# Squaring steps of a recurrent mixer on four TensorE tiles instead of two

## The chip, the cores and the metric

One core of a Trainium2 chip runs the whole kernel. The metric is the device time of one execution in microseconds. TensorE multiplies matrices into PSUM; VectorE (DVE) and ScalarE (ACT) take the products out of PSUM, change them and write them to SBUF; SyncE and GpSimd only move data here. TensorE is used as 64 by 64 tiles in the part that is changed: which half of the partitions an operand lies on gives the tile's row, and which half of the partitions of PSUM the result goes to gives its column, so that there are four tiles, (0,0), (0,1), (1,0) and (1,1).

## What is computed

A two-layer encoder on 512 + 256 tokens of width 1024. A layer is a SwiGLU, a mixer of three kinds of heads, and another SwiGLU. The change is in the first kind of heads, the RWKV-7 scan, four heads of 64 channels, run forward and backward:

```python
def step(s, inp):
    r_t, w_t, k_t, v_t, kk_t, a_t = inp
    s = (s * w_t[:, :, None, :]
         - jnp.einsum('bhij,bhj->bhi', s, kk_t)[..., None] * (kk_t * a_t)[:, :, None, :]
         + v_t[..., None] * k_t[:, :, None, :])
    return s, jnp.einsum('bhij,bhj->bhi', s, r_t)
```

The kernel does it by chunks of 64 tokens. For each chunk and head it needs the inverse of a 64 by 64 triangular matrix. It splits it into blocks of 16 on the diagonal, whose inverse is the product (I+N)(I+N^2)(I+N^4)(I+N^8), and the rest. The squaring steps of this product are what the change touches.

## The kernel before

**Stages.** In each layer the mixer's recurrent part, `rwkv`, runs four passes (`q` = 0 to 3: two directions times two pairs of heads). A pass holds 12 chunks for 2 heads, and goes through eleven steps (`s` = 0 to 10). Each step is done for three groups (`g` = 0, 1, 2) of four chunks one after another, so a pass is 33 calls of `batch(l, q, s, g)`, written once for each engine: the one of TensorE multiplies (L948 on), the ones of ScalarE (L1511 on) and VectorE (L1976 on) take the products out. Group g has the two PSUM banks 2g and 2g+1 for itself.

**Order.** Every engine runs its own list in order. A product of step s waits until VectorE and ScalarE have both finished step s-1 of its group (`rv` and `ra_` at `s - 1`); both of them wait for TensorE's products of their step (`rp`). While group 0 is taken out, TensorE multiplies groups 1 and 2.

**Layouts.** A 64 by 64 matrix of a chunk and a head lies on one half of the partitions. In one layout the half tells the head, in the other the parity of the chunk. `into_pairs` reads the half by head and writes the half by parity, `out_of_pairs` the other way round; both walk over the four tiles of `TILES`. `inside` reads and writes the same half, so it uses the tiles (0,0) and (1,1) alone. `out_of_pairs` can already add a second product to the first in PSUM. In steps 3 to 6 all is in the layout by parity. Step 3 squares (`sq_b`, `sq_a`) and gives N^2 as `M2X[..., 0, :]` and its transpose as `sq_c`; `M2X[..., 1, :]` is the running product X.

- Step 4: from `sq_c` times `M2X`, both parts side by side in 128 columns, bank 2g gets N^4 and the addend to X, and bank 2g+1 the transpose of N^4. ScalarE copies the transpose to `sq_b` (L1520); VectorE copies N^4 to `sq_a` (L2005) and adds the addend to X in SBUF (L2006).
- Step 5: the same once more with `sq_b`, `sq_a`. ScalarE copies the transpose of N^8 to `sq_c` (L1522); VectorE adds to X (L2008).
- Step 6: the last addend, from `sq_c` and X, added by VectorE (L2008).
- Step 7: two `out_of_pairs` calls; ScalarE takes them out in three copies (L1524 to L1526), VectorE waits for the first of them (`turned`), and adds the unit matrix (L2010).

Each of the float32 products appears in the trace as two weight loads and two matmuls.

**Beside the steps.** After group 0 of some steps TensorE has other work (`lora_part` in steps 2 to 5 of passes 0 to 2, `chain_step` in pass 2, means, variances and a "bonus" product in pass 3, from `between`). ScalarE has a sigmoid after each of steps 2 to 5. VectorE computes the next pass's features after steps 6 to 9: `cumulate` (L2025 to L2030) stands right behind step 6 on its list. In pass 3 it has `bonus` (L2143) behind group 0 and three operations on 128x768 (L2132, L2135, L2177) behind steps 4 and 5.

Of the kernel before, what the change touches and what calls it, by code (L numbers as in the profile page):

```python
# [40 lines left out]
CH = 64  # L41
# [3 lines left out]
TILES = ((0, 0), (1, 1), (0, 1), (1, 0))  # L45
# [92 lines left out]
def build(nc, xT, wa, par_d, small_d, const_d, hy_d, hw_d, bias_d, outT):  # L138
# [4 lines left out]
    with ExitStack() as ctx:  # L143
# [617 lines left out]
        def _(pe):  # L761
# [157 lines left out]
                    if i == 0 and s == 0:  # L919
                        norm()  # L920

            def into_pairs(g, n, at, width, lhs, rhs):

                for j in range(2):
                    for h, p in TILES:
                        c, r = 4 * g + 2 * j + p, slice(64 * h, 64 * h + 64)
                        m = mm(ps[64 * p:64 * p + 64, 2 * g + h, width * j + at:width * j + at + n], lhs(c)[r, :], rhs(c)[r, :])
                return m

            def out_of_pairs(g, n, at, width, lhs, rhs, lhs2=None, rhs2=None):  # L930
# [17 lines left out]
            def batch(l, q, s, g):  # L948
# [3 lines left out]
                part = lambda t, a: (lambda c: t[:, c, a, :])  # L952
                parts = lambda t, a, n: (lambda c: t[:, c, a:a + n, :].rearrange("p a t -> p (a t)"))
                vv = lambda v: vtok[:, i, v, :]
                if s:
                    if s - 1 in VECTOR_STAGES:
                        pe.wait_ge(*rv.at(l, "b", q, s - 1, g))
                    if s - 1 in ACT_STAGES:
                        pe.wait_ge(*ra_.at(l, "b", q, s - 1, g))
                elif q:  # L960
                    pe.wait_ge(*rv.at(l, "b", q - 1, BATCH - 1, g))
                    pe.wait_ge(*ra_.at(l, "b", q - 1, BATCH - 1, g))
# [8 lines left out]
                    inside(g, 1, 64, 0, one(sq_a), one(sq_b))  # L971
                    m = inside(g, 1, 64, 256, part(Q, 0), vv)
                elif s == 4:
                    inside(g, 0, 128, 0, one(sq_c), parts(M2X, 0, 2))
                    m = inside(g, 1, 64, 0, part(M2X, 0), one(sq_c))
                elif s == 5:
                    inside(g, 0, 64, 0, one(sq_b), part(M2X, 1))
                    m = inside(g, 1, 64, 0, one(sq_a), one(sq_b))
                elif s == 6:
                    m = inside(g, 0, 64, 0, one(sq_c), part(M2X, 1))  # L980
                elif s == 7:
                    out_of_pairs(g, 64, 192, 256, part(NR, 0), part(M2X, 1))
                    m = out_of_pairs(g, 192, 0, 256, part(M2X, 1), parts(NR, 0, 3))
                elif s == 8:
                    into_pairs(g, 64, 0, 192, one(sq_a), one(sq_b))
                    m = into_pairs(g, 128, 64, 192, part(NR, 0), parts(Q, 0, 2))
                elif s == 9:
                    m = inside(g, 0, 128, 0, one(sq_c), parts(NR, 1, 2))
                else:
                    out_of_pairs(g, 128, 0, 256, part(Q, 0), parts(btok_Mrb, 0, 2))  # L990
                    out_of_pairs(g, 64, 128, 256, part(btok_Mrb, 0), part(Q, 1), one(ktok), vv)
                    m = out_of_pairs(g, 64, 192, 256, part(Q, 1), part(btok_Mrb, 1), vv, one(Mrk))
# [387 lines left out]
        def _(sa):  # L1380
# [130 lines left out]
            def batch(l, q, s, g):  # L1511
# [5 lines left out]
                    sa.copy(sq_c[:, h, :], same(o + 1, 0))  # L1517
                    m = A(NR[:, h, 2, :], ps[:, o + 1, 256:512].rearrange("p (v t) -> p v t", t=CH), ACT.Copy, scale=-1.0)
                elif s == 4:
                    m = sa.copy(sq_b[:, h, :], same(o + 1, 0))  # L1520
                elif s == 5:
                    m = sa.copy(sq_c[:, h, :], same(o + 1, 0))  # L1522
                elif s == 7:
                    sa.copy(outer(sq_b[:, h, :]), quad(o, 256, 192)).then_inc(*ra_.inc(l, "turned", q, g))  # L1524
                    sa.copy(outer(sq_a[:, h, :]), quad(o, 256, 0))
# [222 lines left out]
        def _(ve):  # L1748
# [227 lines left out]
            def batch(l, q, s, g):  # L1976
# [5 lines left out]
                X = M2X[:, h, 1, :]  # L1982
                if s == 7:
                    ve.wait_ge(*ra_.at(l, "turned", q, g))
                else:
                    ve.wait_ge(*rp.at(*k, s, g))
                if s:
# [14 lines left out]
                elif s == 3:  # L2002
                    m = ve.tensor_copy(M2X[:, h, 0, :], same(o, 0))
                elif s == 4:
                    ve.tensor_copy(sq_a[:, h, :], same(o, 0, CH, 2 * CH))  # L2005
                    m = TT(X, X, same(o, CH, CH, 2 * CH), AD)  # L2006
                elif s in (5, 6):
                    m = TT(X, X, same(o, 0), AD)  # L2008
                elif s == 7:
                    m = TT(NR[:, h, 0, :], sq_b[:, h, :], eye_b(4), AD)  # L2010
# [508 lines left out]
```

## Time and profile before

| | |
|---|---|
| median of three executions | 3546.54 us (3543.47 to 3546.89) |
| profiled execution | 3548.5 us, of which its span is 3546.7 us |
| TensorE busy with matmuls | 3405.4 us, 96% of the span |
| VectorE busy | 1797.2 us, 51% |
| ScalarE busy | 978.5 us, 28% |
| mean granted TensorE clock | 0.99 |
| recurrent part | about 846 to 1022 us and 2600 to 2775 us of the span |

A profiled execution lists every instruction with its start, its length and what ended the idle time before it. In the timeline view, instructions of one kind are merged into one row: the row has the first start, the time to the last end, the engine (PE is the matmul side of TensorE, PEld its weight loads, which overlap), the line of the kernel, output and inputs by name, shapes and the count. "<-DVE" in brackets says that a wait for VectorE ended there; "<-issue" means idle time for which the profile shows nothing that was waited for. All products have line L767, that of a helper, and are told apart by the names of their operands.

### The profile page before, as it was taken

What the parts mean: (1) busy time and instruction counts of PE and PEld (TensorE: products, weight loads), DVE (VectorE), ACT (ScalarE), POOL (GpSimd) and SP (SyncE); (2) the same over time, 40 slices, a digit from 0 to 9 for tenths busy, and PEclk for the clock granted to TensorE, in tenths of its full rate; (3) what the DMA queues carried; (4) which work ended last, traced back from release to release, by engine and by line L of the source; (5) the groups of instructions that cost most, each with busy time, mean ns of one, the idle gap of its engine ahead of it and who ended that gap; (6) DMA issues with size and microseconds to landing.
All of it is one profiled execution on the core that took longest, in us unless ns stands there. A gap on an engine that the chain in (4) does not pass through costs nothing.

```text
span 3546.7 us, 60872 instructions
## 1 busy us (share of the span) xinstructions
PE 3405.4 (96%) x26620; PEld 3217.2 (91%) x26620; DVE 1797.2 (51%) x3152; ACT 978.5 (28%) x1607; POOL 50.5 (1%) x62
## 2 busy tenths in 40 slices
PE   7999999999887999999999999999998879999998
PEld 7999999887766999999999999998877669999998
DVE  5443445664878433333454434456448774333334
ACT  4221223222453321211331212232134633221212
POOL 0000000000000000000000000000000000000000
PEclk9999999999998999999999999999999989999999
DMA  3222121231051212212122221222300512122121
GB/s 136 62 70 77 57 72 63 97 109 58 4 196 50 88 54 69 65 62 73 56 78 74 67 76 54 77 96 67 121 26 21 209 48 71 59 71 61 52 72 62
DMA packets 78456, 264.30 MB, mean 75 GB/s; under 512 B 8738, under 2 KB 8738, under 8 KB 76912
## 3 DMA queue, kind: packets, MB, share of 16 engines
q1 hardware_dynamic: 74640, 248.08, 21.2%
q0 software_dynamic: 3552, 12.34, 1.1%
q8 instruction: 210, 3.44, 0.4%
q14 instruction: 54, 0.44, 0.0%
HBM read 230.50 MB, written 29.88 MB: 73 GB/s over the span
## 4 chain that ended last, share of the span: by engine, by line
PE 90%; DVE 6%; ACT 2%; issue 1%; DMA 0%; SPq 0%; DVEq 0%
PE ps L767 89%; DVE uv L2228 1%; PE ps L1285 1%; DVE rstd L1779 0%; DVE sc L2281 0%; DMA x<-xT 0%; DVE Mrk L1995 0%; ACT Q L1526 0%; ACT L1398 0%; DVE xab L2217 0%; DVE btok_Mrb L1991 0%; DVE btok_Mrb L1992 0%; DVE ktok L1996 0%; DVE xab L2218 0%; DVE sc L2292 0%
## 5 line engine op out<-in xcount | busy, mean ns | idle before, releaser
L767 PE MATMUL ps<-hh,wh 128*128 128x384 f32 (+2 forms) x3520 | 1188.8, 338 | 11.9 <-DVE hl L1787 10.9
L767 PE MATMUL ps<-hl,wh 128*128 128x384 f32 (+2 forms) x3520 | 1179.9, 335 | 0.0
L767 PE MATMUL ps<-hh,wl 128*128 128x384 f32 (+2 forms) x3520 | 1179.4, 335 | 0.0
L767 PEld LDWEIGHTS ps<-hh,wh 128*128 128x128 f32 x3520 | 663.5, 188 | 35.5 <-issue 16.5
L767 PEld LDWEIGHTS ps<-hl,wh 128*128 128x128 f32 x3520 | 663.8, 189 | 15.3 <-issue 0.3
L767 PEld LDWEIGHTS ps<-hh,wl 128*128 128x128 f32 x3520 | 663.6, 189 | 14.3
L1413 ACT CAST wh<-wring 128x1024 fp32r<-128x1024 f32 (+2 forms) x372 | 346.1, 955 | 660.8 <-PE ps L767 654.8
L767 PE MATMUL ps<-act_high,wl 128*128 128x384 f32 x1408 | 470.3, 334 | 0.0
L767 PE MATMUL ps<-act_high,wh 128*128 128x384 f32 x1408 | 470.3, 334 | 0.0
L767 PE MATMUL ps<-act_low,wh 128*128 128x384 f32 x1408 | 470.3, 334 | 0.0
L1893 DVE TENSOR_TENSOR silu<-ps,rstd 128x384 f32<-128x384 f32 x176 | 98.0, 557 | 700.7 <-PE ps L767 700.7
L1769 DVE TENSOR_TENSOR wl<-wring,wh 128x1024 fp32r<-128x1024 f32 (+2 forms) x372 | 405.6, 1110 | 71.1 <-ACT wh L1413 68.9
L1817 DVE SCALAR_TENSOR_TENSOR x<-ps,x 128x384 f32<-128x384 f32 x288 | 160.3, 557 | 463.3 <-PE ps L767 463.2
L1470 ACT ACTIVATE silu<-silu 128x384 f32<-128x384 f32 x176 | 92.5, 526 | 1014.1 <-DVE silu L1893 1014.1
L767 PEld LDWEIGHTS ps<-act_high,wh 128*128 128x128 f32 x1408 | 264.3, 188 | 0.0
L767 PEld LDWEIGHTS ps<-act_low,wh 128*128 128x128 f32 x1408 | 264.3, 188 | 0.0
L767 PEld LDWEIGHTS ps<-act_high,wl 128*128 128x128 f32 x1408 | 264.3, 188 | 0.0
L1899 DVE TENSOR_TENSOR act_low<-gated,act_high 128x384 fp32r<-128x384 f32 x176 | 98.3, 559 | 102.6 <-ACT act_high L1474 102.6
L1474 ACT CAST act_high<-gated 128x384 fp32r<-128x384 f32 x176 | 90.2, 513 | 111.2 <-DVE gated L1897 111.2
L767 PE MATMUL ps<-mh,wh 128*128 128x384 f32 x256 | 90.7, 354 | 20.3 <-issue 12.9
L1897 DVE TENSOR_TENSOR gated<-silu,gated 128x384 f32<-128x384 f32 x176 | 98.3, 558 | 23.1 <-ACT silu L1470 0.9
L1894 DVE TENSOR_TENSOR gated<-ps,rstd 128x384 f32<-128x384 f32 x176 | 96.4, 547 | 0.0
(266 smaller groups left out, 3315.9 us busy)
## 6 DMA issues: line engine op xcount, KB each, us to landing
wring<-wa SPq DMA_DIRECT2D x244, 512.0 KB, 3.6
wring<-wa SPq DMA_DIRECT2D x64, 384.0 KB, 3.2
wring<-wa SPq DMA_DIRECT2D x64, 320.0 KB, 3.0
bias<-bias SPq DMA_DIRECT2D x24, 512.0 KB, 7.4
conv_q_k<-stage SPq DMA_DIRECT2D x28, 384.0 KB, 2.6
kern_rows<-kst POOLq DMA_DIRECT2D x12, 512.0 KB, 3.3
outT<-x SPq DMA_DIRECT2D x2, 3072.0 KB, 10.4
kern<-kern_rows SPq DMA_DIRECT2D x12, 512.0 KB, 7.3
```

Source lines behind the costliest of these rows:

```text
L767: return pe.matmul(out, lhsT, rhs, start=start, stop=stop)
L1285: m = pe.transpose(ps[:, 4 + a, P * j:P * j + P], sc[:, n % SCB, 2 * a + j // 2, P * (j % 2):P * (j % 2) + P], cs("ident"))
L1413: sa.copy(wh[:, slot_of(t), 0:k, :], wring[:, t % RAWS, 0:k, :]).then_inc(s_whi, 1)
L1470: A(silu[:, u % 2, :], silu[:, u % 2, :], ACT.Silu).then_inc(s_silu, 1)
L1474: sa.copy(ah[:, j - j0, hf_ * HALF:(hf_ + 1) * HALF], gated[:, u % 2, :]).then_inc(s_ahi, 1)
L1769: TT(wl[:, slot_of(t), 0:k, :], wring[:, t % RAWS, 0:k, :], wh[:, slot_of(t), 0:k, :].bitcast(F32), SU)\
L1817: STT(xs, bank(banks + v % 4, HALF), factor, xs, M, AD).then_inc(s_xup, 1)
L1893: TT(silu[:, u % 2, :], bank(2 * (u % 2), HALF), rstd[:, cols], M).then_inc(s_gate, 1)
L1894: TT(gated[:, u % 2, :], bank(2 * (u % 2) + 1, HALF), rstd[:, cols], M).then_inc(s_up, 1)
L1897: TT(gated[:, u % 2, :], silu[:, u % 2, :], gated[:, u % 2, :], M).then_inc(s_mul, 1)
L1899: TT(al_[:, j - j0, cols], gated[:, u % 2, :], ah[:, j - j0, cols].bitcast(F32), SU)\
L2228: m = TT(uv[:, k, trig, :].rearrange("p (e c) -> p e c", e=2), xab[:, k, :].rearrange("p (e c) -> p e c", e=2), by, M)
```

## The change

Step 4 goes from the layout by parity to that by head, and step 5 back again, so that both run on four tiles. Because X changes layout too, its old value can't be added from SBUF by VectorE: TensorE adds it, as the product of a unit matrix (`eye`) with X that is the first of two in the same PSUM place. `into_pairs` gets the second product that `out_of_pairs` has. VectorE then only copies: both parts of `M2X` in one copy of 128x512 in step 4, X in one of 128x256 in step 5. Since every output now lies in both banks of the group, VectorE waits in these two steps for ScalarE's copy (`ra_` at s, g) and no longer for TensorE itself. The products of step 4 number 32 for a group instead of 16 (8 of which had 128 columns), those of step 5 number 24 instead of 16.

```diff
-            def into_pairs(g, n, at, width, lhs, rhs):
+            def into_pairs(g, n, at, width, lhs, rhs, lhs2=None, rhs2=None):
                 for j in range(2):
-                    for h, p in TILES:
-                        c, r = 4 * g + 2 * j + p, slice(64 * h, 64 * h + 64)
-                        m = mm(ps[64 * p:64 * p + 64, 2 * g + h, width * j + at:width * j + at + n], lhs(c)[r, :], rhs(c)[r, :])
+                    for a, b, first, last in ((lhs, rhs, True, lhs2 is None), (lhs2, rhs2, False, True)):
+                        for h, p in TILES if a else ():
+                            c, r = 4 * g + 2 * j + p, slice(64 * h, 64 * h + 64)
+                            m = mm(ps[64 * p:64 * p + 64, 2 * g + h, width * j + at:width * j + at + n], a(c)[r, :], b(c)[r, :],
+                                   first, last)
...
+                eye = lambda v: cs("eye")
...
                 elif s == 4:
-                    inside(g, 0, 128, 0, one(sq_c), parts(M2X, 0, 2))
-                    m = inside(g, 1, 64, 0, part(M2X, 0), one(sq_c))
+                    out_of_pairs(g, 64, 128, 192, part(M2X, 0), one(sq_c))
+                    out_of_pairs(g, 64, 0, 192, one(sq_c), part(M2X, 0))
+                    m = out_of_pairs(g, 64, 64, 192, eye, part(M2X, 1), one(sq_c), part(M2X, 1))
                 elif s == 5:
-                    inside(g, 0, 64, 0, one(sq_b), part(M2X, 1))
-                    m = inside(g, 1, 64, 0, one(sq_a), one(sq_b))
+                    into_pairs(g, 64, 64, 128, part(M2X, 0), one(sq_b))
+                    m = into_pairs(g, 64, 0, 128, eye, part(M2X, 1), one(sq_b), part(M2X, 1))
...
                 elif s == 4:
-                    m = sa.copy(sq_b[:, h, :], same(o + 1, 0))
+                    m = sa.copy(outer(sq_b[:, h, :]), quad(o, 192, 128))
                 elif s == 5:
-                    m = sa.copy(sq_c[:, h, :], same(o + 1, 0))
+                    m = sa.copy(inner(sq_c[:, h, :]), quad(o, 128, 64))
...
+                elif s in (4, 5):
+                    ve.wait_ge(*ra_.at(*k, s, g))
                 else:
                     ve.wait_ge(*rp.at(*k, s, g))
...
                 elif s == 4:
-                    ve.tensor_copy(sq_a[:, h, :], same(o, 0, CH, 2 * CH))
-                    m = TT(X, X, same(o, CH, CH, 2 * CH), AD)
-                elif s in (5, 6):
+                    m = ve.tensor_copy(outer(M2X[:, h, :, :].rearrange("p c a t -> p c (a t)")), quad(o, 192, 0, 128))
+                elif s == 5:
+                    m = ve.tensor_copy(inner(X), quad(o, 128, 0))
+                elif s == 6:
                     m = TT(X, X, same(o, 0), AD)
```

## Rows read from the trace of the kernel before

**Rows 1.** The page: TensorE's busy time and instructions; the queue that loads instructions.

```profile
PE 3405.4 (96%) x26620; PEld 3217.2 (91%) x26620; DVE 1797.2 (51%) x3152; ACT 978.5 (28%) x1607; POOL 50.5 (1%) x62
...
q8 instruction: 210, 3.44, 0.4%
```

**Rows 2.** Busy time by engine in steps 4 to 6 of passes 0, 2, 3 (stretch, its length, busy us and count of each engine, clock).

```profile
861.00:870.70 9.70, 9.70 (x247) 8.84 (x244) 4.49 (x12) 4.23 (x11) 0.00 (x0) 1.00 0.01 3
...
945.20:955.40 10.20, 10.20 (x264) 9.34 (x262) 5.31 (x15) 4.22 (x11) 0.00 (x0) 1.00 0.01 3
989.50:1003.50 14.00, 13.22 (x256) 10.44 (x252) 11.92 (x23) 3.75 (x10) 0.00 (x0) 1.00 0.05 6
```

**Rows 3.** Timeline of pass 0, layer 0, weight loads: steps 4, 5, 6, 7 begin.

```profile
860.96 0.85 PEld L767 LDWEIGHTS ps<-M2X,sq_c 64*64 64x64 f32 x16
...
862.51 0.29 PEld L767 LDWEIGHTS ps<-pa,small 32*128 32x128 f32 x2
...
863.14 0.85 PEld L767 LDWEIGHTS ps<-M2X,sq_c 64*64 64x64 f32 x16 [0.33 <-issue]
...
864.47 0.85 PEld L767 LDWEIGHTS ps<-M2X,sq_c 64*64 64x64 f32 x16
...
865.81 0.55 PEld L767 LDWEIGHTS ps<-M2X,sq_b 64*64 64x64 f32 x16
...
866.28 0.55 PEld L767 LDWEIGHTS ps<-sq_b,sq_a 64*64 64x64 f32 x16
...
869.38 1.48 PEld L767 LDWEIGHTS ps<-M2X,sq_c 64*64 64x64 f32 x48
...
870.73 0.37 PEld L767 LDWEIGHTS ps<-M2X,NR 64*64 64x64 f32 x16
```

**Rows 4.** The same timeline: step 4 of group 0 taken out, and the wait before step 8.

```profile
862.57 0.37 ACT L1520 COPY sq_b<-ps 128x256 f32<-128x256 f32 x1
862.57 0.43 DVE L2005 COPY sq_a<-ps 128x256 f32<-128x256 f32 x1 [0.92 <-PE ps L767]
862.91 0.41 DVE L2006 TENSOR_TENSOR M2X<-M2X,ps 128x256 f32<-128x256 f32 x1
...
875.12 0.32 PEld L767 LDWEIGHTS ps<-sq_b,sq_a 64*64 64x64 f32 x16 [1.81 <-DVE NR L2010]
```

**Rows 5.** Timeline, weight loads on four tiles, 64 columns, in step 10.

```profile
883.11 0.25 PEld L767 LDWEIGHTS ps<-vtok,ktok 64*64 64x64 f32 x8
883.23 0.25 PEld L767 LDWEIGHTS ps<-btok_Mrb,Q 64*64 64x64 f32 x8
```

**Rows 6.** Groups by line and shape (count, busy us, mean ns); VectorE behind ScalarE in pass 3.

```profile
L2012 DVE TENSOR_TENSOR Q<-NR,ps 128x512 f32<-128x512 f32 x12 | 8.2, 686 | 5.4 <-PE ps L767 5.2
...
1004.70 0.37 ACT L1524 COPY sq_b<-ps 128x256 f32<-128x256 f32 x1 [2.16 <-PE ps L767]
...
1005.10 0.43 DVE L2010 TENSOR_TENSOR NR<-sq_b,cst 128x256 f32<-128x256 f32 x1 [0.98 <-ACT sq_b L1524]
```

**Rows 7.** Timeline of pass 3: VectorE in step 5, TensorE at the start of step 7.

```profile
998.55 0.41 DVE L2008 TENSOR_TENSOR M2X<-M2X,ps 128x256 f32<-128x256 f32 x1
...
1003.51 0.33 PEld L767 LDWEIGHTS ps<-M2X,NR 64*64 64x64 f32 x16 [0.94 <-DVE M2X L2008]
```

**Rows 8.** TensorE's unexplained stops in steps 8 and 10, and stretches between such stops.

```profile
886.13 0.33 PE L767 MATMUL ps<-btok_Mrb,Q 64*64 64x128 f32 x2 [0.36 <-issue]
...
883.22:886.13 2.91, 2.55 (x142) 2.31 (x135) 2.91 (x8) 0.00 (x0) 0.00 (x0) 1.00 0.02 6
...
1011.92:1015.66 3.74, 3.39 (x128) 3.31 (x128) 2.21 (x5) 0.00 (x0) 0.00 (x0) 1.00 0.05 14
1015.66:1019.13 3.47, 2.30 (x128) 2.16 (x128) 1.33 (x4) 0.74 (x2) 0.00 (x0) 1.00 0.02 5
886.13:927.02 40.89, 34.96 (x1017) 29.95 (x1016) 32.67 (x75) 18.20 (x40) 0.00 (x0) 1.00 0.02 4
...
2765.37 0.67 PE L767 MATMUL ps<-Q,NR 64*64 64x128 f32 x16 [1.11 <-issue]
```

## The prediction

> **What bounds the kernel now.** I read the page first, then the windows of the recurrent part, then its timeline. The page says that TensorE is busy 96% of the span [rows 1], but the change touches only steps 4 and 5 of eight passes, so the question is what bounds these. The windows of the three kinds of passes answer it [rows 2]: in pass 0 TensorE is busy for all 9.70 us of steps 4 to 6 and VectorE for 4.49, in pass 2 for all 10.20 us; in pass 3 VectorE is busy 11.92 of 14.00 us and TensorE has gaps. Pass 1 looks like pass 0, and layer 1 repeats layer 0. So in six passes of eight TensorE's own time in these steps is the path; in the two last it is mostly VectorE. Behind step 6 the path changes: step 8 waits 1.81 us for L2010 of VectorE [rows 4], which stands behind `cumulate`. What counts is therefore when VectorE has added the last group's step 6. An earlier end of step 6 moves all that follows, for nothing later in the pass has a clock of its own.
>
> **Part 1: the products.** In pass 0 a group's step 4 takes 864.47 - 863.14 = 1.33 us, and half of a step 5 takes 866.28 - 865.81 = 0.47 us, so 0.93 for a group [rows 3]. On four tiles, eight weight loads, which is four products of 64 columns, follow each other by 883.23 - 883.11 = 0.12 us (0.116 over a longer run of such rows): 0.029 us for a product [rows 5]. Half of these were second products adding in PSUM, so the adding costs nothing extra. The new step 4 is 32 x 0.029 = 0.93 us, the new step 5 is 24 x 0.029 = 0.70 us. That saves 0.40 + 0.23 = 0.63 us for a group, 1.9 us for a pass. The unit-matrix products are in this sum: 8 for a group and step, 0.23 us each time.
>
> **Part 2: the taking out.** ScalarE's copies keep their size, 0.37 us [rows 4]. VectorE had 0.34 (862.91 - 862.57) + 0.41 us for step 4 [rows 4] and gets one operation of 128x512; the nearest row with that size is 686 ns [rows 6]. A copy of 128x256 and an addition of that size take the same (0.43 and 0.41), so I take 0.69 for the copy; bounds 0.60 and 0.75. Step 5 stays at 0.42. The new wait puts VectorE behind ScalarE. The nearest rows are L1524, ending at 1005.07, and L2010, starting at 1005.10 [rows 6]: 0.03 us. A group's way from its last product to the next step becomes about 0.1 + 0.37 + 0.03 + 0.69 = 1.2 us in step 4 and 0.1 + 0.37 + 0.03 + 0.42 = 0.9 in step 5, plus some 0.2 until a product's end is seen. What hides it are the other two groups' products: 2 x 0.93 = 1.9 us in step 4, enough. Behind step 5 the third group has only the first two of step 6, 2 x 0.45 = 0.9 us (three groups take 870.73 - 869.38 = 1.35 [rows 3]) against 1.1: 0.2 us late once a pass. Queued behind the waiting VectorE instruction are the next group's copy and, in pass 2, a state step; none is urgent by more than this. ScalarE's sigmoid stands behind group 2 of the step before and can hold group 0's copy back by up to 0.4 us, which two other groups' products still cover. So in passes 0 and 1 the net is 1.9 - 0.2 = 1.7 us. In pass 2 a state step of 0.65 us on VectorE lies between step 6's additions, and I take 1.5.
>
> **Part 3: pass 3.** There VectorE sets the end: it is busy 11.92 of 14.00 us [rows 2], its addition of step 5 for group 0 comes only at 998.55, and step 7 waits for its addition of step 6 until 1003.51 [rows 7]. It gains only by having less idleness in step 4: groups 0 and 1 come from TensorE 0.4 us earlier each (0.8), of which the wait for ScalarE takes a little back. I take 0.75 us; bounds nothing and 1.0.
>
> Without anything else the sum is 2 x (1.7 + 1.7 + 1.5 + 0.75) = 11.3 us.
>
> **Part 4: the supply of instructions.** The change adds instructions where they already run fastest. TensorE's 53,240 instructions came in 210 packets [rows 1], about 254 for each. In step 10, the densest code now, TensorE stops in the middle of a group with nothing awaited, as at 886.13 [rows 8]. These stops are a whole number of 256 instructions apart: exactly 128 + 128 between those at 1011.92, 1015.66 and 1019.13, and 1017 + 1016 between 886.13 and 927.02, which with some 15 semaphore instructions makes 8 x 256 [rows 8]. So they fall where one packet's instructions end and the next begin, and only where the packet before was used up fast. From the last such border to the end of the stop I read 2.91, 3.74 and 3.47 us [rows 8]; there are ten such stops in the two layers' recurrent parts, the first at 886.13; for eight of them it is 2.7 to 3.75, for two that lie beside large transfers 5.9 and 6.0 (one of these ends at 2765.37 [rows 8]). Borders with 3.5 us or more of work between them mostly pass without a stop. I take 3.2 us as the least time of a packet.
>
> Now 256 instructions take 3.7 us in step 3 (14.6 ns each, 32 for 0.47 us) and lie under no such limit. In the new steps 4 and 5 a product is 4 instructions in 0.029 us, 7.3 ns each: 256 of them take 1.9 us, and 2.6 if they include the projection between, which costs 863.14 - 862.51 = 0.63 and about 0.15 for the array to empty (860.96 to 862.51 is 1.55 us for a group in front of it, not 1.33) [rows 3]. Steps 4 to 6 hold 384 + 288 + 96 instructions, three packets, so two borders whose packet lies wholly inside. Each would stop TensorE by 3.2 - 2.6 = 0.6 us; after a stop the next comes later (3.47 and 3.74 are such), up to 1.0. I take 1.2 us for a pass, bounds 0.5 and 2.0. In pass 3 the bonus products (1.5 us) thin the code and VectorE is the bound: nothing. A pass grows by 3 x (64 + 32) = 288 instructions, so the borders fall elsewhere in each pass, in step 10 too; there the stops now sum to about 8 us over eight passes, and I expect the same number, give or take 3 us.
>
> So passes 0 and 1 keep 1.7 - 1.2 = 0.5 us each, 2.0 over the four of them; pass 2 keeps 1.5 - 1.5 = 0, since it can have a whole packet without the projection in it; pass 3 gives 2 x 0.75 = 1.5. **The sum is 3.5 us.** The profiled execution (span 3546.7, 3548.5 in all) would have 3545.0; from the median of the runs, 3546.5, it is **3543.0 us**.
>
> The Trainium skill, "Runtime: NRT & Kernel Launch", section "Instruction fetch mechanics", says that instructions come in blocks of 256 and that crossing a border is "mostly hidden". The block size agrees with the rows; that it is hidden does not, by stops like the one of 1.11 us at 2765.37 [rows 8]. By its word the sum would be rival A's.
>
> The page "TensorEngine Tiling (Array Packing)", section "PSUM Bottleneck", warns that after a fourfold speedup the PSUM copies may become the bound. That is rival C; the trace has no step in which they do at 0.70 us for a group.
>
> **The rivals.**
> A. **No stops of supply in steps 4 to 6**, or ones that the waits swallow. For it: step 7 and step 8 run on four tiles without a stop, though followed or preceded by waits. Then 11.3 us: 3535.2. Chance 0.25.
> B. **Supply costs more than the products gain: slower.** If a packet takes 4.3 us where two dense ones follow each other (between the quiet 3.75 and the 5.9 beside transfers), a pass loses 2 x 1.7 = 3.4 against 1.7, six passes lose 10 us and pass 3 gives 1.5 back: 3555. It decides from 3.5 us for a packet on, where gain and loss are even. Against it: only the two stops beside transfers were that long. Chance 0.08.
> C. **The copies become the bound**: both copies of a group in a row, 0.37 + 0.42 us, are longer than its 0.70 us of products in step 5. They belong to two engines, so the rate is that of the slower, 0.42, and only the last group's latency shows. If the two don't overlap between groups, each group of step 5 waits another 0.1 to 0.2 us and step 4's 0.1: 0.8 us a pass, six passes 5 us less gain than A, 3540, or none at all beside the main case's stops: 3547. Chance 0.12.
> D. The change doesn't do what it says: if tiles of two columns kept the old rate of 0.058 us for a product, step 4 would be 1.9 us; rows 5 exclude that. Chance 0.
>
> **How the numbers follow.** Main case 0.55, from 3540 to 3547 by the bounds of 0.5 and 2.0 us a pass and the 3 us of step 10. A 0.25, C 0.12, B 0.08. The range that leaves out half of A's tail and B: 3536 to 3550. A measurement of this kernel tells about 0.2%, 7 us, from no change. Faster by more than that: most of A and a little of the main case, 0.27. Slower by more: B, 0.06. Within: 0.67.
>
> **What would show it.** In the new trace: weight loads of `eye` rows in steps 4 and 5 at 0.12 us for eight; step 4 of a group in 0.93 us and step 5 in 0.70 where there is no stop; L2005's successor at 0.69 us, 0.03 behind ScalarE's copy; new "<-issue" stops of 0.5 to 1.0 us inside steps 4 and 5, spaced by 256 instructions, at other places in each pass. If steps 4 to 6 of pass 0 take 8.0 us or less instead of 9.75 with no such stops, A is right and I am wrong; if they take over 9.7, B.

## The result, and the profile of the changed kernel

The changed kernel takes 3554.5 us (median of 14 runs, 3549.2 to 3559.2), the kernel before 3548.0 us beside it (14 runs, 3543.5 to 3553.9). The ratio is 1.0017, with a 95% interval of 1.0009 to 1.0024: slower by 0.17%, some 6 us, where a gain of 3.5 us was forecast. 3554.5 us lies above the range of 3536 to 3550 us. Two executions, one of e10_before_extras (3819.8 us) and the profiled one of e6_noeye (14.7 ms), were disturbed and are left out of the numbers below. The profiled execution of the new kernel has a span of 3555.1 us, that of before 3546.7.

The page, first and third part, answers to [rows 1]: 1152 more weight loads and as many more matmuls, 9 more packets of instructions.

```profile
PE 3398.3 (96%) x27772; PEld 3205.8 (90%) x27772; DVE 1794.1 (50%) x3128; ACT 977.5 (27%) x1607; POOL 50.4 (1%) x62
...
q8 instruction: 219, 3.59, 0.4%
```

The unit matrix is kept in the tile `cst`, so its products are shown with `cst`. The timeline of pass 0 in layer 0, steps 4 to 7, answers to [rows 3, 4]. Its columns are start and length in us, engine, line, operation, operands, count, and in brackets the idle time before it with what ended it.

```profile
862.37 0.38 ACT L1524 COPY sq_b<-ps 128x256 f32<-128x256 f32 x1
862.54 0.29 PEld L767 LDWEIGHTS ps<-pa,small 32*128 32x128 f32 x2 [0.54 <-ACT tmp L1505]
...
862.79 0.69 DVE L2011 COPY M2X<-ps 128x512 f32<-128x512 f32 x1 [1.10 <-ACT sq_b L1524]
863.17 0.32 PEld L767 LDWEIGHTS ps<-sq_c,M2X 64*64 64x64 f32 x16 [0.33 <-issue]
...
863.63 0.21 PEld L767 LDWEIGHTS ps<-M2X,cst 64*64 64x64 f32 x8
...
863.75 0.21 PEld L767 LDWEIGHTS ps<-M2X,sq_c 64*64 64x64 f32 x8
...
864.10 0.33 PEld L767 LDWEIGHTS ps<-sq_c,M2X 64*64 64x64 f32 x16
...
866.13 0.29 PEld L767 LDWEIGHTS ps<-pa,small 32*128 32x128 f32 x2 [0.31 <-ACT tmp L1505]
...
867.75 0.21 PEld L767 LDWEIGHTS ps<-M2X,cst 64*64 64x64 f32 x8 [0.44 <-issue]
...
869.87 0.54 PEld L767 LDWEIGHTS ps<-M2X,sq_c 64*64 64x64 f32 x16 [0.16 <-DVE M2X L2013]
...
871.60 0.13 PEld L767 LDWEIGHTS ps<-M2X,NR 64*64 64x64 f32 x1 [0.95 <-issue]
```

The parts of the sum are there: a group's step 4 takes 864.10 - 863.17 = 0.93 us, eight loads follow the eight before by 0.12, the copy takes 0.69 us and starts 0.04 behind ScalarE's. So are the stops with nothing awaited, which end at 867.75 and 871.60. Two things are there that no part of the sum has: TensorE waits for `tmp` of ScalarE at 862.54 and 866.13, and one of the stops lies in step 7.

The same timeline behind step 7 (L1528 is L1524 of before, L2017 is L2010, L1533 is L1529):

```profile
872.61 0.37 ACT L1528 COPY sq_b<-ps 128x256 f32<-128x256 f32 x1 [2.88 <-PE ps L767]
...
874.66 0.33 PEld L767 LDWEIGHTS ps<-sq_b,sq_a 64*64 64x64 f32 x16 [0.67 <-DVE NR L2017]
...
875.86 1.28 ACT L1402 ACT_TABLE_LOAD   x1
...
880.40 4.26 PEld L767 LDWEIGHTS ps<-NR,sq_c 64*64 64x64 f32 x48 [3.74 <-ACT NR L1533]
```

In the timeline of before, beside 875.12 for step 8 [rows 4]:

```profile
871.97 0.38 ACT L1524 COPY sq_b<-ps 128x256 f32<-128x256 f32 x1 [1.57 <-PE ps L767]
...
875.21 1.28 ACT L1398 ACT_TABLE_LOAD   x1
...
879.76 2.60 PEld L767 LDWEIGHTS ps<-NR,sq_c 64*64 64x64 f32 x48 [2.64 <-ACT NR L1529]
```

TensorE's step 8 is 0.46 us earlier than before, with VectorE's result for which it waits; ScalarE's chain is 0.65 us later, and step 9 follows ScalarE.

The windows (stretch, length, busy us and count by engine, granted clock, DMA share, GB/s) of two packets of instructions, then of step 9 in passes 0 and 1, layer 0:

```profile
867.75:871.60 3.85, 3.01 (x127) 2.74 (x127) 2.47 (x7) 1.12 (x3) 0.00 (x0) 1.00 0.01 4
910.44:913.96 3.52, 3.00 (x127) 2.72 (x127) 1.51 (x4) 1.12 (x3) 0.00 (x0) 1.00 0.02 5
880.40:884.50 4.10, 4.10 (x44) 4.10 (x46) 1.56 (x3) 1.47 (x4) 0.00 (x0) 0.58 0.00 0
922.90:925.50 2.60, 2.53 (x48) 2.53 (x52) 2.47 (x4) 1.54 (x5) 0.00 (x0) 1.00 0.00 0
```

The first two run from the end of one stop to the end of the next: 127 + 127 instructions and two for semaphores, a packet each. The third is step 9 at a mean granted clock of 0.58: most of it ran at 0.50, the lower of the two levels (1.2 GHz). The fourth has the same products at 1.00 (2.4 GHz).

For all eight passes I cut each timeline at the same events: the start of VectorE's addition of step 2, TensorE's first product of step 7, of step 9 and of step 10, and the start of VectorE's last operation of step 10. The table has the sums over the eight passes in us, for before, after and every experiment below by its label. "Stops" are number and sum of all stops over 0.15 us at a packet's end in these stretches; the few at which TensorE waits for another engine as well are counted in.

```
                    steps 2-6   steps 7-8   step 9   step 10   sum      stops
before              136.0       68.0        25.0     48.8      277.8    10: 8.1
after               136.7       72.8        27.4     48.8      285.8    28: 22.4
after, again        135.4       72.3        29.0     50.5      287.1    26: 20.1
e1_wait             137.7       68.0        25.3     49.1      280.0     9: 9.0
e2_shift128         141.2       67.4        30.4     50.1      289.1    29: 24.6
e3_warm             137.0       72.4        22.7     50.5      282.6    27: 22.2
e4_wide             129.8       71.3        27.4     50.1      278.6    24: 15.8
e5_lean             131.6       69.7        22.8     51.4      275.5    25: 18.3
e7_lora1            142.3       70.3        25.6     50.0      288.2    29: 25.0
e8_all              128.7       69.7        22.8     50.6      271.8    23: 17.3
e9_noeye_again      120.2       68.4        27.7     49.8      266.1    12: 8.9
e10_before_extras   136.1       67.3        23.1     49.1      275.6    12: 10.8
e11_before_shift    136.0       67.6        25.8     50.7      280.1    11: 9.6
```

**What the stops wait for** can be read from the same traces. They date every packet of the instruction queue (16,384 bytes each), though the views printed here only sum them. The packet ahead of the stop that ends at 867.75 moved from 865.29 to 866.17, that ahead of 871.60 from 869.14 to 870.02: both stops end 1.58 us after a packet has landed. In the 13 traces of the table, 224 of 230 stops over 0.25 us at a packet's end with nothing else awaited end 1.2 to 1.6 us after a landing. The other six are a pause of 0.33 us that also stands at 863.17, where no packet ends. The second packet began to move 1.39 us after the stop before it had ended (867.75), took 0.88 us, and needed 1.58 more: that makes the 3.85 us of the first window above.

The change adds 0.7 us to steps 2 to 6, 4.8 to steps 7 and 8 and 2.4 to step 9. Outside these stretches the two profiled executions take 3269.3 us and 3268.9.

### The profile page after: what moved, and what is told of

Same layout as the page of the kernel before. It is cut to its first block, busy times and chain, and to the rows that moved or that the text cites. A ratio compares the mean times of both kernels' runs of the same rounds, so it can differ in the third digit from the quotient of the medians.

```text
span 3555.1 us, 63152 instructions
## 1 busy us (share of the span) xinstructions
PE 3398.3 (96%) x27772; PEld 3205.8 (90%) x27772; DVE 1794.1 (50%) x3128; ACT 977.5 (27%) x1607; POOL 50.4 (1%) x62
## 4 chain that ended last, share of the span: by engine, by line
PE 90%; DVE 6%; ACT 2%; issue 1%; DMA 0%; SPq 0%; DVEq 0%
PE ps L767 89%; DVE uv L2235 1%; PE ps L1289 1%; DVE rstd L1783 0%; DVE sc L2288 0%; DMA x<-xT 0%; DVE Mrk L2001 0%; DVE sc L2299 0%; ACT Q L1530 0%; ACT L1402 0%; DVE xab L2224 0%; DVE btok_Mrb L1997 0%; DVE btok_Mrb L1998 0%; DVE xab L2225 0%; DVE ktok L2002 0%
## 5 line engine op out<-in xcount | busy, mean ns | idle before, releaser
L1901 DVE TENSOR_TENSOR gated<-silu,gated 128x384 f32<-128x384 f32 x176 | 98.2, 558 | 22.7 <-ACT silu L1474 0.5
```

The lines of the kernel that those rows point to most:

```text
L1901: TT(gated[:, u % 2, :], silu[:, u % 2, :], gated[:, u % 2, :], M).then_inc(s_mul, 1)
```

## Experiments

Two theories stood against each other at first. **S, the supply of instructions:** the gain of the products is there and is eaten by stops where one packet of 256 TensorE instructions ends. **C, the copies:** VectorE's new wait behind ScalarE and its copy of 128x512 hold up TensorE. With the profile of after came a third, **the clock:** a longer idleness before step 9 lets the clock fall.

**The wait alone, in the kernel before** (e1_wait).

```diff
+                elif s in (4, 5):
+                    ve.wait_ge(*ra_.at(*k, s, g))
                 else:
                     ve.wait_ge(*rp.at(*k, s, g))
```

> The kernel before, with one part of the change alone: in steps 4 and 5 VectorE waits for ScalarE's copy instead of for TensorE. Products and instruction count are those of before. Theory S (the change loses its gain to TensorE's supply of instructions): the wait is covered by the other groups' products but for the last group of step 5, 0.2 to 0.4 us a pass, so +1 to +3 us in all, and the stops stay where they are in the kernel before. Theory C (the loss is that the taking out now runs one engine behind the other): most of the loss of 6.5 us appears here already.

Measured 3552.3 us, 1.0010 [1.0001, 1.0019] of before: a median 3.7 us longer, more than the 1 to 3 us of S. In the trace the recurrent part is longer by only 2.2 us, steps 2 to 6 by 1.6: 0.21 us a pass in passes 0 and 1, nothing in pass 2, 0.4 in pass 3. The rest of that execution's extra time lies outside the recurrent part, where the code is the same. Timeline, the wait behind ScalarE and its one result on TensorE a pass:

```profile
863.46 0.37 ACT L1520 COPY sq_b<-ps 128x256 f32<-128x256 f32 x1
863.87 0.42 DVE L2007 COPY sq_a<-ps 128x256 f32<-128x256 f32 x1 [1.32 <-ACT sq_b L1520]
...
868.41 0.54 PEld L767 LDWEIGHTS ps<-M2X,sq_b 64*64 64x64 f32 x16 [0.33 <-DVE M2X L2008]
```

So where the edit acts the wait costs what S gave it, and not most of the 6.5 us that C needed. C is out as the main cause by the trace; the medians alone would not settle it.

**Other places for the packets' ends, in the changed kernel** (e2_shift128): 32 products that nobody reads (128 instructions) behind layer 0's projections, ahead of its recurrent part.

```diff
+                if l == 0:
+                    pe.wait_ge(*ra_.at(l, "sig", 0, 3))
+                    pe.wait_ge(*rv.at(l, "vt", 1))
+                    for _ in range(8):
+                        for h, p in TILES:
+                            r = slice(64 * h, 64 * h + 64)
+                            mm(ps[64 * p:64 * p + 64, 6 + h, 0:64], cs("eye")[r, :], cst[r, 0:64])
```

> The changed kernel with 128 more TensorE instructions (32 products of a unit matrix that nobody reads) once, in the wait ahead of layer 0's recurrent part. They cost at most 0.2 us there. Theory S: every unexplained stop of TensorE moves, to borders that fall 128 instructions earlier in the code, still whole multiples of 256 apart; the time changes by up to 4 us either way, since other work stands at the borders. Theory C: the stops belong to the code where they are and stay; the time stays within 1 us of the changed kernel.

Measured 3558.1 us, 1.0027 [1.0016, 1.0039]. Half a packet more ahead of the part, and the stops lie elsewhere, in the timeline of pass 0:

```profile
867.08 0.14 PEld L767 LDWEIGHTS ps<-M2X,cst 64*64 64x64 f32 x3 [1.01 <-issue]
...
871.12 0.13 PEld L767 LDWEIGHTS ps<-M2X,sq_b 64*64 64x64 f32 x1 [1.31 <-issue]
...
875.20 0.13 PEld L767 LDWEIGHTS ps<-M2X,NR 64*64 64x64 f32 x1 [0.35 <-issue]
```

The stop in the second group of step 5 (ending at 867.75 in after) has become one in its first group, the one in step 7 has become one at the end of step 5, and the next falls to the end of step 7 and is smaller. Steps 7 and 8 are as short as before again (67.4 us against 68.0), and steps 2 to 6 are 4.5 us longer than in after: 4.7 us more of stops, and in pass 1 of layer 1 a stretch at the lower clock behind a stop of 1.49 us (more on this at e7_lora1). A stop belongs to a place in the stream of instructions, not to a product. Counted over all of TensorE's instructions, those for semaphores included, in every kernel here it is an instruction of the same remainder by 256 that comes late.

**The clock** (e3_warm): two products of 128x512 behind step 8 in passes 0 and 1, to shorten TensorE's idleness.

```diff
+                            if s == 8 and g == 2 and q < 2:
+                                for _ in range(2):
+                                    mm(bank(6), cs("ident"), cst[:, 0:512])
```

> The changed kernel with two extra products of 128x512 (read by nobody) behind step 8 in passes 0 and 1, where TensorE is idle for 2.7 to 3.8 us and in two of the four passes came back at half the clock: step 9 then took 4.3 us instead of 2.6. Theory K (part of the loss is the clock that falls in this idle time): step 9 is back at 2.6 us in all passes, the kernel 3 us faster than the changed one. If the clock is not a cause: no change, or up to 1 us slower for the added work.

Measured 3551.6 us, 1.0008 [0.9998, 1.0018]. Timeline, a stop in step 7 as in the changed kernel, and step 9:

```profile
871.21 0.13 PEld L767 LDWEIGHTS ps<-M2X,NR 64*64 64x64 f32 x1 [0.68 <-issue]
...
880.01 2.60 PEld L767 LDWEIGHTS ps<-NR,sq_c 64*64 64x64 f32 x48 [2.14 <-ACT NR L1536]
```

Step 9 is short in all four passes with the added products, and its sum falls from 27.4 to 22.7 us. The clock's share is real, and it is not a property of the change alone. The kernel before has it once in this trace, after the usual 2.64 us of idleness:

```profile
2633.02 4.26 PEld L767 LDWEIGHTS ps<-NR,sq_c 64*64 64x64 f32 x48 [2.64 <-ACT NR L1529]
```

In passes 0 and 1 of both layers, step 9 took over 3.4 us, against 2.46, in 7 of 16 cases in before, e1, e9 and e11, in 16 of 20 in the changed kernel, its repetition (e12), e2, e4 and e7, and in none of 16 where the two products were added (e3, e5, e8, e10). By the length of the idleness right ahead of step 9 it was 12 of 22 after 2.64 us, and 11 of 14 after longer ones (2.8 to 3.7 us).

**Fewer instructions for the same step 4** (e4_wide): the identity is added to whole products of two columns, 24 products instead of 32 for a group.

```diff
                     out_of_pairs(g, 64, 128, 192, part(M2X, 0), one(sq_c))
-                    out_of_pairs(g, 64, 0, 192, one(sq_c), part(M2X, 0))
-                    m = out_of_pairs(g, 64, 64, 192, eye, part(M2X, 1), one(sq_c), part(M2X, 1))
+                    for j in range(2):
+                        for first in (True, False):
+                            for p, h in TILES:
+                                v, r = 4 * g + 2 * h + j, slice(64 * p, 64 * p + 64)
+                                a, n = (0, 2) if first else (1, 1)
+                                m = mm(ps[64 * h:64 * h + 64, 2 * g + p, 192 * j + 64 * a:192 * j + 128],
+                                       (one(sq_c) if first else eye)(v)[r, :], parts(M2X, a, n)(v)[r, :], first, not first)
```

> The changed kernel with step 4's second and fourth set of products joined: sq_c times both parts of M2X in 128 columns, then the unit-matrix product added to the second half. 24 products for a group instead of 32, 96 instructions instead of 128; the same result, array time 0.86 us instead of 0.93 for a group. Theory S: 96 instructions fewer a pass, over a third of a packet that takes 3.2 to 3.8 us at least: 0.8 to 1.2 us a pass in six passes, 5 to 7 us faster than the changed kernel, about the kernel before. Theory C and array time alone: 0.2 us a pass, 1.3 us faster.

Measured 3549.9 us, 1.0006 [0.9996, 1.0015]. Timeline, step 4 of group 1 and the first of group 2, then the one stop in step 5:

```profile
861.81 0.32 PEld L767 LDWEIGHTS ps<-sq_c,M2X 64*64 64x64 f32 x16 [0.33 <-issue]
...
862.21 0.26 PEld L767 LDWEIGHTS ps<-M2X,cst 64*64 64x64 f32 x8
...
862.71 0.33 PEld L767 LDWEIGHTS ps<-sq_c,M2X 64*64 64x64 f32 x16
...
867.15 0.21 PEld L767 LDWEIGHTS ps<-M2X,cst 64*64 64x64 f32 x8 [0.55 <-issue]
```

A group's step 4 takes 862.71 - 861.81 = 0.90 us against 0.93: the products save 0.7 us in all (24 x 0.03). Yet steps 2 to 6 are 6.9 us shorter than in after. Its stops in steps 3 to 6 sum to 2.4 us, of which 0.8 is at a place where TensorE waits for VectorE as well, those of after to 9.6, and this difference of 7.2 us is the gain, less some that new waits take back. The same arithmetic in nearly the same time on the array, a quarter fewer instructions in one step, and the time goes with the instructions. Fewer instructions also move all the packets' ends, which alone can be worth some us (e2). But the two kernels with this step 4 and the projection in its place have 129.8 and 131.6 us in steps 2 to 6 (e4, e5), the four with the step 4 of after 135.4 to 141.2 (after, e12, e3, e2). By the medians the kernel is 4 to 5 us faster than the changed one, where 5 to 7 were expected.

**The two together** (e5_lean).

> The changed kernel with both: step 4 in 24 products for a group, and the two extra products behind step 8 that keep TensorE from idling. Theories S and K together, taken as independent: 4 to 6 us from fewer instructions and 3 to 4 us from the clock, so 7 to 10 us faster than the changed kernel and 1 to 3 us faster than the kernel before.

Measured 3545.6 us, 0.9993 [0.9983, 1.0002]; steps 2 to 6 131.6 us, step 9 22.8 us, both about as in the single runs. It can't be told from the kernel before: the interval has 1 in it.

**No unit products at all** (e6_noeye, e9_noeye_again). Here the old value is not added: steps 4 and 5 have the four-tile products and copies, but the running product is lost, and the time is that of the rest.

```diff
-                    m = out_of_pairs(g, 64, 64, 192, eye, part(M2X, 1), one(sq_c), part(M2X, 1))
+                    m = out_of_pairs(g, 128, 0, 192, one(sq_c), parts(M2X, 0, 2))
...
-                    m = into_pairs(g, 64, 0, 128, eye, part(M2X, 1), one(sq_b), part(M2X, 1))
+                    m = into_pairs(g, 64, 0, 128, one(sq_b), part(M2X, 1))
```

> The changed kernel without the unit-matrix products, so the running product's old value is not added: this part of the computation is left out. Steps 4 and 5 have 16 products for a group each, as many instructions as the kernel before (64 and 64), but on four tiles: array time 0.62 and 0.46 us for a group instead of 1.33 and 0.93. Theory S: with a packet's 256 instructions spread over about 3 us again the stops in steps 4 to 7 shrink from about 12 us to under 4 us, and steps 3 to 6 of passes 0 to 2 become 1.5 to 2.5 us shorter than before each, 9 to 15 us in all. If instead the new wait behind ScalarE or the copies were the bound, they would stay near the changed kernel's length, at most 0.5 us a pass shorter.

Measured 3536.5 us, 0.9962 [0.9950, 0.9975]. It left no trace that can be compared, so the same kernel ran again:

> The changed kernel without the unit-matrix products once more (it leaves out adding the running product's old value), for a usable trace. Theory S: 10 to 13 us faster than the kernel before; steps 3 to 6 sum to 122 to 127 us over the eight passes instead of 136.0; stops there under 4 us; no group of 256 instructions in less than 2.7 us.

Measured 3534.7 us, 0.9964 [0.9951, 0.9977]. The page's instruction queue and the loads of step 4, group 1 to step 5:

```profile
q8 instruction: 210, 3.44, 0.4%
```

```profile
863.15 0.33 PEld L767 LDWEIGHTS ps<-sq_c,M2X 64*64 64x64 f32 x16 [0.33 <-issue]
...
863.77 0.38 PEld L767 LDWEIGHTS ps<-sq_c,M2X 64*64 64x64 f32 x16
...
873.12 0.33 PEld L767 LDWEIGHTS ps<-sq_b,sq_a 64*64 64x64 f32 x16 [1.81 <-DVE NR L2016]
```

As many instructions as before, on four tiles, 863.77 - 863.15 = 0.62 us for a group's step 4, and in steps 4 to 7 of all eight passes one stop of 0.30 us. The fastest 256 instructions in steps 2 to 6 took 3.5 us. Steps 7 and 8 take 68.4 us and the idle time before step 8 is 1.81 us again. Steps 2 to 6 take 120.2 us, below the 122 to 127 expected. Against after, 16.5 us are gone from them: the unit products' own time, 8 x 3 x 2 x 0.23 = 11 us, and 9.6 us of stops, less some 4 us by which TensorE's waits for the sigmoid have grown (8.7 us against 4.6). So the unit products cost 16.5 us, more than four tiles without them give (136.0 - 120.2 = 15.8), and a third of it, 5.5 us, is not array time.

**TensorE's wait for the sigmoid** (e7_lora1). In after, TensorE waits 4.6 us in all in steps 2 to 6, in before not at all: `lora_part` behind group 0 waits for L1505 of ScalarE, which reads what it overwrites. Here it stands behind group 1.

```diff
-                        if g == 0 and q < 3 and s in LORA_AT:
+                        if g == 1 and q < 3 and s in LORA_AT:
...
+                            if g == 1 and s in LORA_AT and q < 3:
+                                lora_part(l, q + 1, LORA_AT[s])
                             if g == 0:
-                                if s in LORA_AT and q < 3:
-                                    lora_part(l, q + 1, LORA_AT[s])
                                 between(l, q, s)
```

> The changed kernel with the next pass's projection behind group 1 instead of group 0 in steps 2 to 5. In the changed kernel TensorE waits 0.5 us in step 4 and 0.3 us in step 5 of pass 0 there for ScalarE's sigmoid of the step before. If that wait costs time by itself: it goes, 0.5 to 0.8 us a pass in six passes, 3 to 5 us. By theory S most of it comes back as longer stops, since the same 256 instructions can't go faster than their packet: 0 to 2 us.

Measured 3556.7 us, 1.0022 [1.0012, 1.0031]: no gain, where even S had given it 0 to 2 us. Timeline of pass 0, the projection without a wait, the next stop, and two rows of step 5 behind it; then the window of these:

```profile
863.78 0.29 PEld L767 LDWEIGHTS ps<-pa,small 32*128 32x128 f32 x2
...
868.72 0.14 PEld L767 LDWEIGHTS ps<-M2X,cst 64*64 64x64 f32 x3 [1.82 <-issue]
...
870.41 0.35 PEld L767 LDWEIGHTS ps<-M2X,cst 64*64 64x64 f32 x8
870.62 0.35 PEld L767 LDWEIGHTS ps<-M2X,sq_b 64*64 64x64 f32 x8
```

```profile
870.00:872.00 2.00, 2.00 (x61) 1.97 (x62) 0.06 (x1) 0.35 (x2) 0.00 (x0) 0.50 0.00 0
```

The wait is gone and the stop behind it is 1.82 us long; all stops in steps 2 to 6 sum to some 5 us more than in after, about what the waits had been. So far S holds: a wait taken out of a stretch bound by supply comes back as a stop. But steps 2 to 6 are 5.6 us longer than in after, and the stops don't explain that. Soon after the stop the granted clock is 0.50, and eight loads follow the eight before by 0.21 us instead of 0.12. This happened in three passes, 0 and 1 of layer 0 and 1 of layer 1, behind stops of 1.82, 1.79 and 2.24 us. These three are 6.0 us longer than in after, the other five 0.5 us shorter. About 12 us of steps 2 to 6 ran at the lower level; at 0.21 for 0.12 that costs some 5 us (an estimate). A long stop can thus cost twice, by its own time and by the clock behind it; that the stop brings the clock down is read from these rows and has no experiment of its own. The only other stop of over 1.4 us in steps 2 to 6 of any kernel, 1.49 us in e2, was followed by the lower clock too; one of 1.77 us in step 10 of e3 was not.

**All three edits** (e8_all).

> The changed kernel with all three: 24 products in step 4, the extra products behind step 8, and the projection behind group 1. Theory S: within 2 us of the one with the first two. If the wait for the sigmoid counts by itself: 3 us faster than that one, 4 to 6 us faster than the kernel before.

Measured **3541.2 us** (3539.5 to 3542.9), 0.9979 [0.9970, 0.9989]: faster than both kernels. That is 4.4 us faster than the last one (e5), outside the 2 us of S: the wait for the sigmoid does count by itself. With the instructions of step 4 down, the same move of the projection now gives 2.9 us in steps 2 to 6 (131.6 to 128.7), and no stretch of the recurrent part runs at the lower clock. Timeline of pass 0:

```profile
869.49 0.21 PEld L767 LDWEIGHTS ps<-M2X,cst 64*64 64x64 f32 x8 [1.05 <-issue]
...
880.64 2.60 PEld L767 LDWEIGHTS ps<-NR,sq_c 64*64 64x64 f32 x48 [1.62 <-ACT NR L1541]
```

Stops remain, 17.3 us in all.

**Is it the four tiles, or the two small edits?** (e10_before_extras) The kernel before with the products behind step 8 and the projection behind group 1:

> The kernel before with the two things that were added to the changed one beside the joined products: the two extra products behind step 8 in passes 0 and 1, and the projection behind group 1. In the kernel before one of four such passes came back at half the clock (1.7 us) and the projection waited for nothing. If the gain of the combined version comes from the four tiles: this one gains 0 to 2 us against the kernel before, not 7. If it comes from the extras: 4 to 7 us.

Measured 3547.0 us, 0.9994 [0.9985, 1.0004]; recurrent part 275.6 us against 271.8 for e8. Its step 9 is as short as e8's, its steps 2 to 6 are those of before. So e8's lead, 5.7 us by the medians, is that of the lean four tiles. The traces show 3.8 us of it: 136.1 - 128.7 = 7.4 us in steps 2 to 6 and 0.3 in step 9, less 2.4 in steps 7 and 8 and 1.5 in step 10. The other 2 us are not located.

**Are the ends of packets harmless in the kernel before?** (e11_before_shift) The same 128 instructions as in e2, put ahead of its recurrent part:

> The kernel before with the same 32 products ahead of layer 0's recurrent part, which move the packet borders by 128 instructions. Theory S: its stops, ten with 8 us in step 10 and beside it, move to other instructions and change in size; sum 6 to 11 us, the time within 3 us of the kernel before. Steps 3 to 6 stay at 15.63 us in passes 0 and 1, for there no 256 instructions take under 3.5 us.

Measured 3549.6 us, 1.0005 [0.9995, 1.0014]. Steps 2 to 6 are 136.0 us as before to 0.1, with no stop at a packet's end in them that waits for nothing else; in step 10 of pass 0 the stop has moved:

```profile
887.87 0.20 PEld L767 LDWEIGHTS ps<-Mrk,vtok 64*64 64x64 f32 x4 [0.93 <-issue]
```

In steps 2 to 6, whose fastest 256 instructions take over 4 us, the supply keeps up in both placements of the packets' ends; in step 10 it doesn't.

**The changed kernel again** (e12_after_again, "after, again" in the table), to see what repeats:

> The changed kernel as it is, once more beside these. Theory S: its stops stand at the same instructions as in the first trace, since the code is the same, while their sizes differ by some tenths of a us; the sum in steps 3 to 10 is 20 to 25 us. Ratio to the kernel before 1.001 to 1.0025.

Measured 3554.8 us, 1.0019 [1.0009, 1.0028]. Timeline of pass 0, the same two stops, 1.2 us later than in the first trace:

```profile
868.94 0.21 PEld L767 LDWEIGHTS ps<-M2X,cst 64*64 64x64 f32 x8 [0.81 <-issue]
...
872.78 0.13 PEld L767 LDWEIGHTS ps<-M2X,NR 64*64 64x64 f32 x1 [0.95 <-issue]
```

Same instructions, similar lengths: the places repeat from execution to execution, a single length varies by some tenths. The sums of the table vary by 1.3 us in steps 2 to 6 and by 1.6 to 1.7 in steps 9 and 10 between the two executions; smaller differences between kernels with many stops should not be read.

## Why the prediction was wrong

The mechanism that it named for a loss, stops of supply, was right. What failed is what it put at nothing: stops behind step 6 (4.8 us), TensorE's wait for the sigmoid (3.7 us) and the clock (2.4 us).

**Part 1 was right:** 0.93 and 0.70 us for a group, eight loads in 0.12.

**Part 2 was right in its prices and wrong in what covers them.** Copy 0.69 us, 0.04 behind ScalarE, 0.16 us late once a pass: as forecast, and e1 confirms the wait alone at 0.2 us a pass. "ScalarE's sigmoid [...] can hold group 0's copy back [...], which two other groups' products still cover" named the right instruction and the wrong victim. The sigmoid reads what `lora_part` overwrites, so TensorE itself waits for it. Group 0 and the start of the projection take 862.54 - 860.94 = 1.60 us, before 1.55 [rows 3], where 0.40 should have been gained; in step 5 another 0.18 is lost. Without its stop of 0.52 us, pass 0 gains 15.63 - 15.14 + 0.52 = 1.0 us; passes 0 and 1 of both layers gain 3.6 us by this measure instead of 6.8, pass 2 gives 2.5 instead of 3.0. The term is short by 3.7 us; the waits for the sigmoid sum to 4.6.

**Part 3 was right to a little:** passes 3 gain 0.7 and 0.5 us, their new stops included, against 0.75 each: 0.3 us short.

**Part 4 was right in kind and right in size where I looked, and stopped looking one step too early.** The stops of passes 0 to 2 inside steps 3 to 6 sum to 8.0 us, forecast 7.8. That they agree so well is in part luck: a packet took 3.4 to 4.2 us there and not the 3.2 that I took, and the waits for the sigmoid, which I had put at nothing, filled 0.5 to 0.8 us a pass that would else have been stops (e7). Step 10 keeps its length (48.8 us both), and the stops there stay within the 3 us. The Trainium skill, "Runtime: NRT & Kernel Launch", section "Instruction fetch mechanics", has the block of 256 right, as every run here shows; its "mostly hidden" holds for steps 2 to 6 before (also in e11) and fails for the same steps after, with 0.2 to 1.4 us at nearly every border.

**This is the step that failed most.** The packet that ends behind step 6 is also dense, and its border lies in step 7: stops of 1.03, 0.96, 0.24 and 0.88 us. I had written "What counts is therefore when VectorE has added the last group's step 6", since step 8 waits for VectorE [rows 4]. That made a stop in step 7 free. It was read from one wait. The stop doesn't touch VectorE's `cumulate`, but it delays the results that ScalarE copies, and behind these nine copies stand the table load, three exponentials, and the copies on which step 9 waits. Steps 7 and 8 grow by 1.09, 0.81, 0.16 and 1.07 us in those four passes, and by 1.64 in pass 3 of layer 0, whose stop fell into step 8 (1.60 us): 4.8 us. e9, with no such stops but one of 0.3, has 68.4 us there, before 68.0.

**The clock was no part of the sum:** 2.4 us in step 9. That the added products take this away is shown (e3, 4.7 us less in step 9). That the stops made the lower clock more frequent is likely from 16 of 20 cases against 7 of 16, no more; the longer idleness ahead of step 9 is not the whole of it, since 12 of 22 cases after the same 2.64 us had it as well. The 2.4 us are the most accidental part of the account: the repetition has 4.0.

The account in the profiled executions: forecast -3.5 us; + 3.7 for the wait behind the sigmoid, + 0.5 for stops in steps 3 to 6 and pass 3, + 4.8 for steps 7 and 8, + 2.4 for the clock = +7.9 us, as measured (285.8 - 277.8).

**Rival B** had the right sign and the right mechanism, and a different size of it: packets of 4.3 us inside steps 4 to 6. Packets took 3.4 to 4.2, and the rest of the loss lay behind step 6. Its sign, steps 4 to 6 of pass 0 over 9.7 us, did not come (9.34 us), but passes 1 have 10.6 and 10.5. At 0.08 its chance was too low. By the prediction's own measure of 7 us for a difference that can be told, 6.5 us is still "within"; the interval from more runs excludes no change. **Rival A** fell with the first stop. **Rival C**: the wait alone is 1.6 us (e1), and in the new trace TensorE waits for a copy of VectorE by 0.16 us a pass. The Trainium skill, "TensorEngine Tiling (Array Packing)", section "PSUM Bottleneck", says that the copies may become the bound. Here they don't: in steps 2 to 6 of after TensorE waits 3.2 us in all for the copies of steps 4 and 5 (L2011, L2013), and 9.6 us for instructions.

Open: what sets the least time of a packet. It ranges from 2.6 to 4.2 us in these stretches. The transfer itself took 0.9 to 1.3 us at the stops of after, and 1.3 to 1.6 more passed until TensorE went on. What differs most is how long after the previous packet's end the transfer begins (0.1 to 1.7 us at most of these stops), and the traces don't say why. In the two cases of 5.9 us in before, which the prediction put beside large transfers, the packet itself took 1.1 us and began 3.4 and 3.5 us after the border. Open too is how much of the 4 us between e5 and e8, and between after and e2, is only where the borders happen to fall.

## What to carry to other kernels

Where a step moves to four tiles with products of 64 columns, count instructions as well as array time: at 7 ns an instruction TensorE uses up 256 in less time than the next 256 take to come, and an extra pass through the array (here the unit product in place of an addition on an engine with time to spare) is paid in array time and again in stops. Prefer wider products for the same work, and don't remove a wait inside such a stretch before the instructions are fewer: the stop that comes in its place can take the clock down with it. Before a stop is called hidden, follow every engine that reads the stopped step's results, not only the one whose wait ends last in the profile of before.

## What was unexpected of the hardware

- Stops at a packet's end add up: 8.1 us in ten before, 22.4 in 28 after, for 9 more packets out of 219. After a stop the next packet is often as slow or slower (3.36, then 3.84 us in pass 0).
- Joining products, a quarter fewer instructions in one step and 0.7 us less array time, gave 6.9 us in its stretch (e4).
- A stop ends 1.2 to 1.6 us after its packet of instructions has landed, in 224 cases out of 224.
- Behind stops of 1.5 to 2.2 us amid dense code TensorE went on at 0.50 of its clock (three times in e7, once in e2).
- Step 9 runs at a mean granted clock of 0.58 or at 1.00 after the same 2.64 us of idleness, 4.26 or 2.60 us for the same 48 loads, and two products of 128x512 in the gap settled it in all 16 cases.
